# A two-block network on one core: the attention's value products moved beside another unit's scores, twelve fillers in its tail, wider sums in the opening, a token-major last block

## The reference

```python
for gi, (window, dilation) in enumerate(((128, 1), (512, 4), (2048, 16))):   # per group
    q = apply_partial_rope(proj[:, :, gi, 0], cos, sin) * scale
    k = apply_partial_rope(proj[:, :, gi, 1], cos, sin)
    o_g, lse_g = dilated_group_attention(q, k, proj[:, :, gi, 2], window, dilation)
wts = jax.nn.softmax(jnp.stack(lses, axis=0), axis=0)
o = jnp.einsum('gbsh,gbshd->bshd', wts, jnp.stack(outs, axis=0))
...
u = jax.nn.relu(rmsnorm(x, norm_ffn) @ w_ff1)
return x + (u * u) @ w_ff2
```

## Time and profile before

| | us |
|---|---|
| median of 3 runs | 3054.78 (3050.89 to 3054.91) |
| the profiled execution | 3049.26 |
| its span, first to last instruction | 3047.6 |
| PE busy | 3011.1 (99%) |
| DVE busy | 1563.9 (51%) |
| ACT busy | 1137.8 (37%) |

### The profile page before, as it was taken

How to read it: one execution, slowest core, us unless ns; L and a number is a source line. 1 busy time by engine, 2 the same in 40 slices (tenths; PEclk the granted TensorE clock), 3 DMA queues, 4 the chain that set the end, 5 groups by cost and what they waited for, 6 DMA issues and landing times.

```text
span 3047.6 us, 39602 instructions
## 1 busy us (share of the span) xinstructions
PE 3011.1 (99%) x16986; PEld 2529.7 (83%) x16986; DVE 1563.9 (51%) x2167; ACT 1137.8 (37%) x1683; POOL 30.3 (1%) x44
## 2 busy tenths in 40 slices
PE   7999999999999999999999999999999999999999
PEld 6888988888987777988889777888889877898887
DVE  7776654545165565633335755653334654663342
ACT  5654422224232333522225455342233455442231
POOL 0000000000000000000000000000000000000000
PEclk9999999999999999999999999999999999999999
DMA  8433354532332221232322221222222221222222
GB/s 298 163 117 106 121 197 152 189 119 84 97 92 67 68 75 61 67 97 97 97 89 87 83 70 57 82 98 96 98 96 90 84 83 64 81 91 97 97 97 83
DMA packets 219917, 311.59 MB, mean 102 GB/s; under 512 B 12032, under 2 KB 120544, under 8 KB 219744
## 3 DMA queue, kind: packets, MB, share of 16 engines
q1 hardware_dynamic: 208528, 267.01, 26.7%
q0 software_dynamic: 10880, 41.95, 3.9%
q10 hardware_dynamic: 336, 0.12, 0.0%
HBM read 306.93 MB, written 2.10 MB: 101 GB/s over the span
## 4 chain that ended last, share of the span: by engine, by line
PE 90%; DVE 7%; ACT 1%; issue 1%; DMA 0%; ACTq 0%; SPq 0%; DVEq 0%
PE G L2067 64%; PE G L2110 9%; PE G L2071 6%; DVE yT L1585 1%; PE X L2175 1%; PE X L2451 1%; DVE w_lo L1220 1%; PE G L2327 1%; PE G L2089 1%; PE X L2528 1%; PE X L2512 1%; PE X L2535 1%; PE X L2292 1%; PE X L2298 1%; PE X L2477 1%
## 5 line engine op out<-in xcount | busy, mean ns | idle before, releaser
L2067 PE MATMUL G<-u_hi,w_hi 128*128 128x512 f32 x2160 | 863.8, 400 | 0.0
L2067 PE MATMUL G<-u_hi,w_lo 128*128 128x512 f32 x2160 | 842.5, 390 | 0.0
L2067 PE MATMUL G<-u_lo,w_hi 128*128 128x512 f32 x2160 | 841.3, 389 | 0.0
L1220 DVE TENSOR_TENSOR w_lo<-raw,w_hi 128x2048 fp32r<-128x2048 f32 (+3 forms) x240 | 540.3, 2253 | 480.5 <-ACT w_hi L640 479.8
L640 ACT CAST w_hi<-raw 128x2048 fp32r<-128x2048 f32 (+3 forms) x242 | 454.6, 1880 | 526.6 <-DMA raw<-in_w_ff 242.4
L2067 PEld LDWEIGHTS G<-u_hi,w_hi 128*128 128x128 f32 x2160 | 405.5, 188 | 101.6 <-issue 18.2
L2067 PEld LDWEIGHTS G<-u_hi,w_lo 128*128 128x128 f32 x2160 | 405.3, 188 | 87.3
L2067 PEld LDWEIGHTS G<-u_lo,w_hi 128*128 128x128 f32 x2160 | 406.1, 188 | 80.1 <-issue 1.4
L2067 PE MATMUL G<-ff_hi,w_hi 128*128 128x512 f32 x448 | 174.9, 390 | 0.0
L2067 PE MATMUL G<-ff_hi,w_lo 128*128 128x512 f32 x448 | 174.4, 389 | 0.0
L2067 PE MATMUL G<-ff_lo,w_hi 128*128 128x512 f32 x448 | 174.3, 389 | 0.0
(11 more groups left out here) (427 smaller groups left out, 4379.6 us busy)
## 6 DMA issues: line engine op xcount, KB each, us to landing
raw<-in_w_ff SPq DMA_DIRECT2D x128, 512.0 KB, 4.4
raw<-in_ffn_w_in SPq DMA_DIRECT2D x88, 512.0 KB, 4.5
ada_raw<-in_ada_w POOLq DMA_DIRECT2D x40, 1024.0 KB, 6.6
raw<-in_w_in SPq DMA_DIRECT2D x56, 512.0 KB, 4.2
raw<-in_attn_w_in SPq DMA_DIRECT2D x96, 256.0 KB, 3.7
raw<-in_ffn_w_out SPq DMA_DIRECT2D x40, 512.0 KB, 4.8
raw<-in_hgrn_w_in SPq DMA_DIRECT2D x32, 512.0 KB, 4.5
raw<-in_attn_w_in SPq DMA_DIRECT2D x24, 512.0 KB, 4.2
```

The source lines that it names most:

```text
L1220: tt(w_lo[slot][:, 0:nk, 0:w], raw[slot][:, 0:nk, 0:w], w_hi[slot][:, 0:nk, 0:w].bitcast(F32), ALU.subtract).then_inc(s_lo, 1)
L2067: ins = mm(G[0:c1_ - c0, m, :], w[iw][:, k, c0:c1_], xs[ix][:, x0(b) + kk, :], start=first, stop=last, skip_group_check=True)
```

## The change

Four places.

1. Opening. Part 0 also leaves its first two k-rows to PE. The sums are 64 columns wide, parts 0 and 1 go to bank G3. Only the first of the four k-tiles of the first weight chunk is split before the adds, the others after; the same in halves for the second chunk. DVE writes `u_full` of tiles 0 and 4, ACT copies tiles 4 to 7 of x into `hT`. Tile 7 of the normed x goes through bank X3. The sum of part 3 comes after the first chunk.
2. Dilated attention. Values at +3, behind the next unit's scores and ahead of the transposes, groups 1 and 2 first and group 0 last; scaling at +4, output transpose at +5, copy at +6. Rotations at offsets 7, 8, 10, 11. In the tail 12 pieces of 6 matmuls: the first chunk of `at_out` in eight, and two of four k-tiles of the second in four. `out_last` does the last two k-tiles for all tiles.
3. Window attention. Values at +6, behind another unit's scores; copy at +7.
4. Last block. Its second half (features 512 to 1023) is token-major, and the residual enters its sum by four transposes of `hT` per tile. ACT copies a finished tile straight to `x_view`. Tiles 0 to 3 are transposed together at one tick. The output goes in one piece of 1 MB and four of 256 KB.

```diff
-        att_last = att_start(ATT_TILES - 1) + 8
+        att_last = att_start(ATT_TILES - 1) + 7
...
-        FIRST_ADA, FIRST_SUMS = (0, 2, 1, 3), (3, 2, 3, 2)
-        ON_PE = {1: 2, 2: 2}
+        FIRST_ADA, FIRST_SUMS = (0, 2, 1, 3), (G[:, 3, 0:256], G[:, 3, 256:512], X[:, 3, 0:256], X[:, 2, 0:256])
+        ON_PE = {0: 2, 1: 2, 2: 2}
+        FIRST_COLS = 64
...
-            pieces = ((0, 4), (4, 6), (6, 7), (7, 8))
-            for k0, k1 in pieces:
-                sp.wait_ge(s_res, k1)
...
+            sp.wait_ge(s_res, 4)
+            sp.dma_start(by_token[:, :, 0:512], x_view[:, :, 0:512]).then_inc(s_out, 16)
+            for j in range(TB):
+                sp.wait_ge(s_res, 5 + j)
+                sp.dma_start(by_token[:, j, 512:1024], x_view[:, j, 512:1024]).then_inc(s_out, 16)
...
+                if k % 4:
+                    sc.activation(u_full[:, k, :], tmp[:, k, :], ACT.Identity, **kw)
                 n.give(sc.activation(u_hi[:, k, :], tmp[:, k, :], ACT.Identity, **kw), s_uhi)
+                if k == 5:
+                    first_h((6, 7))
+                if k == 0:
+                    sc.copy(w_hi[0][:, 1:4, :], raw[0][:, 1:4, :]).then_inc(s_hi, 1)
+                    normed(7)
+                    act.wait_ge(s_free["act"], 4)
                 if k == 3:
+                    first_h((4, 5))
                     first_w(1)
...
-            first_products(0, range(8))
+            first_products(0, range(2, 8))
             first_products(1, range(2, 8))
+            n.take(st["first_k_upper"])
+            n.give(tt(w_lo[0][:, 0, :], raw[0][:, 0, :], w_hi[0][:, 0, :].bitcast(F32), ALU.subtract), st["first_k_lower"])
+            dve.wait_ge(s_asum, 2)
             first_add(0)
-            first_w(0)
             first_add(1)
             first_mix(0)
+            n.take(st["normed_copied"], 3)
+            first_x(0)
             first_u(0)
+            dve.wait_ge(s_hi, 1)
+            tt(w_lo[0][:, 1:4, :], raw[0][:, 1:4, :], w_hi[0][:, 1:4, :].bitcast(F32), ALU.subtract).then_inc(s_lo, 1)
...
-                        p, tau = divmod(T - 7 - 2 * j - part, ATT_TICKS)
+                        p, tau = divmod(T - 7 - 3 * j - part, ATT_TICKS)
...
-            OUT_TICKS = (97, 101, 104, 107)
+            OUT_TICKS = (97, 97, 100, 101, 103, 104, 106, 107, 109, 112, 114, 115)
...
+                        joined = spec is not None and name == order[-1]
+                        if joined and s == 0:
+                            for f in range(4):
+                                nc.tensor.matmul(G[:, m, blk(f)], hT[:, 4 + f, blk(m)], ident, start=f == 0, stop=False, is_transpose=True, skip_group_check=True)
...
-                for t in att_at(T, 6):
+                for t in att_at(T, 5):
...
+                for t in att_at(T, 3):
...
+                    pe.wait_ge(at["copied"], t + 1)
+                    for g in (1, 2):
+                        for r in range(4):
+                            mm(X[32 * r:32 * r + 32, t % 2, 0:P], pt[0:w1, P * (nb + g - 1) + 32 * r:P * (nb + g - 1) + 32 * r + 32],
+                               at_v[0:w1, r, cols(g)], start=g == 1, stop=False, skip_group_check=True, tile_position=(0, 32 * r))
+                    for j in range(nb):
+                        ins = mm(o, pt[:, blk(j)], at_v[:, i - nb + 1 + j, cols(0)], start=False, stop=j == nb - 1, skip_group_check=True)
+                    ins.then_inc(at["output"], 1)
...
-                for t in att_at(T, 4):
...
+            def out_piece(i):
...
+                s, m = (0, i // 2) if i < 8 else (1, i - 8)
+                k0 = 2 * (i % 2) if s == 0 else 0
...
+            def out_last():
...
+                for k in (2, 3):
+                    pe.wait_ge(split_done, base + 4 + k + 1)
+                    for m in range(4):
+                        for iw, ix in PASSES:
+                            ins = mm(G[:, m, :], w[iw][:, k, blk(m)], xs[ix][:, 4 + k, :], start=False, stop=(k, iw, ix) == (3, 1, 0), skip_group_check=True)
+                        if k == 3:
+                            ins.then_inc(s_tile, 1)
...
-                for u in win_at(T, 5):
...
+                for u in win_at(T, 6):
...
-                k = {24: 0, 25: 1, 26: 2, 27: 3, 30: 4, 31: 5}.get(t)
-                if k is not None:
-                    result_tile(k)
+                if t == 24:
+                    for k in range(4):
+                        result_tile(k)
```

More of the change, by code:

```diff
@@ L1287, in first_mix, with first_x @@
                 n.give(stt(mix[:, k0:k0 + 4], mod[:, 8 + k0:12 + k0], 1.0, cols_b[:, k0:k0 + 4], ALU.add, ALU.mult), st["mix"])
+            def first_x(k):
+                n.own(st["mix"])
+                link(ts(u_full[:, k, :], tmp[:, k, :], mix[:, k:k + 1], mod[:, k:k + 1], ALU.mult, ALU.add))
             def first_u(k):
@@ L2020, in linear @@
                         last_k_apart(name, b, x_hi, x_lo, x0, tick)
+                    elif name == "at_out" and b == 0:
+                        out_last()
                     else:
-                        plain(name, b, x_hi, x_lo, tiles, x0, range(1 if name == "at_out" and b == 0 else 0, g["chunks"]), tick=tick)
+                        plain(name, b, x_hi, x_lo, tiles, x0, range(g["chunks"]), tick=tick)
                     ada = ada_index(name, b)
@@ L2062, in plain @@
                                 for iw, ix in PASSES:
[L2063 removed]
+                                    first = kk == 0 and (iw, ix) == (0, 0) and (part is None or part is spec[0]) and not joined
                                     last = kk == last_k and (iw, ix) == (1, 0)
@@ L2502, in window @@
             def window(T):
-                for u in win_at(T, 5):
-                    t, i = divmod(u, 4)
-                    kv, keys = t // 2, keys_of(i)
-                    n.take(ws["copied"])
-                    if i == 0 and u:
-                        n.take(ws["done"])
-                    for j, kb in enumerate(keys):
-                        for a_ in range(2):
-                            ins = mm(X[64 * a_:64 * a_ + 64, 3, blk(i)], z_v[:, kb, 64 * kv:64 * kv + 64], win_pt[u % 2][:, blk(a_ * len(keys) + j)],
-                                     start=i == 0, stop=kb == i, skip_group_check=True, tile_position=(0, 64 * a_))
-                    if i == 3:
-                        n.give(ins, ws["output"])
                 for u in win_at(T, 0):
@@ L2530, in window @@
                     n.give(ins, ws["scores"])
+                for u in win_at(T, 6):
+                    t, i = divmod(u, 4)
+                    kv, keys = t // 2, keys_of(i)
+                    if i == 0 and u:
+                        n.take(ws["done"])
+                    for j, kb in enumerate(keys):
+                        for a_ in range(2):
+                            ins = mm(X[64 * a_:64 * a_ + 64, 3, blk(i)], z_v[:, kb, 64 * kv:64 * kv + 64], win_pt[u % 2][:, blk(a_ * len(keys) + j)],
+                                     start=i == 0, stop=kb == i, skip_group_check=True, tile_position=(0, 64 * a_))
+                    if i == 3:
+                        n.give(ins, ws["output"])
                 for u in win_at(T, 3):
```

153 lines of the change are left out of this document (93 added, 60 removed).

## The result

The changed kernel takes 3033.94 (median of 4 runs, 3033.12 to 3034.33) against 3052.84 for the kernel before beside it (4 runs, 3050.45 to 3054.91): ratio 0.9941, 95% interval 0.9928 to 0.9953. Forecast were 3034.5 and 3024 to 3045. The profiled execution took 3033.12, its span is 3031.4, 16.2 shorter than before.

The account below looks back on a forecast made before the run. TensorE (PE), busy 99% of the span, was taken as the bound. Gains of 2.0 + 8.8 + 5.0 + 3.6 + 1.1 = 20.5, taken from the median 3054.78, gave 3034.5, range 3024 to 3045.

Parts of the forecast that it names:

- Opening: Start of kernel: first projection at 27.3 instead of 30.49, second block at 57.4 instead of 59.41; gain 2.0.
- The chain that follows (ada sums, scans) has over 1 us to spare: After the opening: work behind the second block has over 1 us of slack, so the opening's 2.0 gain stands.
- Rival B: Opening: the clock falls at 25.2 despite 64-column sums; gain 19.1 in all, time 3035.7; chance 0.20.
- Like units: Attention under the projection: changeovers per unit fall from 0.58 to 0.15, 0.40 saved in each of 12 units.
- Unlike units: Attention under the projection, values of 32 or 64 rows: one more changeover of 0.12, so 0.28 saved in 13 units.
- the order's leftovers: Attention under the projection: an allowance that took the 8.4 from 25 units to 8.8.
- C: Unlike narrow tiles in attention and window pay 0.43 per changeover: 13 less, gain 7.4, time 3047.4; chance 0.12.
- E: Any step from scores to values drains PE; slower kernel, 3062.8 at 0.5 more per step; chance 0.03.
- Rival D: Output transposes under the projection wait 0.6 for DVE in each of 25 units: gain 5.5, time 3049.3; chance 0.05.
- Attention end: From unit 26's scores to the second block: 49.5 becomes 44.4, with stalls 1.6, 0.8 and 1.3; gain 5.0.
- Window: Window attention, values behind scores: 0.15 saved in 13 of 16 units, 0.05 lost in up to 3; 3.6 for two layers.
- Last block: Last block and output: last matmul 0.87 later, shorter way to the copy, output 0.2 faster; gain 1.1.

Follow-up runs that it names:

- e9: Changed kernel with the last four products of ada_w's eighth part over 16 of 512 columns; first scores 830.5 after the second block, no total time given.
- e10: Changed kernel with the attention end's three waits removed and the first window scores waiting only for the first half of the rotated queries; 3026.72, ratio 0.9916.
- e1: Changed kernel with opening sums one column wide in place of 64; second block starts at 58.30 against 58.76, no total time given.
- e2: Changed kernel with 24 more identity transposes issued before the first transposes of x; projection started at 29.92 against 29.20, no total time given.
- e4: Changed kernel with the narrow value products over 128 rows everywhere; the run took 3035.2.
- e3: Changed kernel with the values at their new place but full tiles first and narrow ones last; 3042.43, ratio 0.9967.
- e12: Kernel before, unchanged, run a third time for another profile; 3051.67.

## Why the prediction was right

Every part went the way that was forecast, and the time was right within 0.6, but the latter by errors that nearly cancel. The sum was 4.3 too large against the profiled executions (20.5 for 16.2). Against it, the kernel before usually runs 3 longer than in its profiled execution (3049.26, below all of its 32 timed ones, whose median is 3052.3), the changed kernel only 0.8; and the median that the gain was taken from, 3054.78, lies 1.9 above the one measured beside the change. That the time came so near is luck. (Less 20.5 that median is 3034.3, not the 3034.5 written, and the fifth k-tile's start adds up to 45.3, not 45.5.)

- **Opening, forecast 2.0.** The step that failed is "The chain that follows (ada sums, scans) has over 1 us to spare". The spare was 1.4 in the profile before, already less than the 2.0 that was to come off in front of it; it is 0.4 in the changed kernel's own profile and gone in six other executions [e9, e10]. e9 shows that VectorE's work ahead of the scans sets it; that the transfers of `ada_w` time that work is in part argued. The second block started 2.2 earlier in e10, and the first scores 0.1. In the profiles the first scores start at 889.79 to 891.69 with the opening of before (five) and at 889.31 to 891.87 with the new one (seven; e2 and e9 are left out): no difference that they show. Of the projection's 1.9 of lateness, 0.6 is a later start of that execution (the products began at 15.63, not 15.05); for the rest PE's own sums stood last (they ended at 26.8, not 25.1), since part 0's and most of the transposes behind them ran at the lower clock (3.68 and 4.76 long, in e10 2.00 and 3.55). e10 shows nearly the forecast's times where they didn't.
- **The clock.** With one column it fell at 24 to 26.3 in all six profiles. With 64 it held in seven of eight and fell in e10, behind a wait of 0.93 between the sums that the seven don't have. So the width made the difference in seven executions and was not enough in the eighth. Rival B's fall is real, but it costs nothing that reaches the first scores: e1 and e10 have it and start them at 889.45 and 889.79. The Trainium skill (TensorE: Matmul & The Clock Gate, Part 4) has transposes not counted as busy. e2 speaks against it once more: only transposes stood before the sixteen that ran 0.11 apart.
- **Like units, 0.40.** Measured 0.37. Narrow to full costs 0.22 in all (0.12 on the last narrow group, 0.10 on the first full matmul, and 0.08 on the projection less 0.08 ahead of it), not 0.15.
- **Unlike units, 0.28.** Measured 0.18 and 0.20. The changeover itself is 0.12 to 0.15 by e4, where 0.12 was assumed, and only 32 and 64 rows pay it. Twelve like units at 0.37 and thirteen unlike at 0.19 make the 6.9, where the forecast's prices make 8.4; the 0.4 that it added for "the order's leftovers" stood on no row and didn't come. Rivals C and E fall: C's place is right, at a third of its price. The Trainium skill (TensorEngine Tiling (Array Packing), Key Properties) has the array drained when the tiling mode changes, not when only the tile does. The runs agree: from 128 rows to 96 in narrow tiles nothing is paid, to 64 or 32 it is 0.12 to 0.15.
- **Rival D.** No wait of PE on the output transposes under the projection: the 0.6 of margin was enough.
- **Attention end, 5.0.** Waits are 3.2 where 3.7 were placed, but PE's own work is 42 and not 40.6: each of the twelve pieces starts with a matmul of 0.32 in place of 0.23, which is 1.0 of it.
- **Window, 3.6.** Measured 3.2. Per unit it is 0.13, where 0.15 was forecast, and 2.1 a layer up to the last unit's scores; 0.45 is then lost where the last units' values stand by themselves (0.15 was allowed).
- **Last block, 1.1.** With the forecast in brackets, eight transposes more cost 0.84 (0.87), the shorter way to the copy gives 1.85 (1.77), the output 0.28 (0.2, which no row of before had shown).

## What to carry to other kernels

Small matmuls of different tile shapes cost by the border, not by the piece: put the narrow ones of one unit directly behind the narrow ones of another, with rows that cost no changeover (96 beside 128 cost none, 32 and 64 did), and keep one passage to the full array. The same move with the full tiles first is worth 0.4 of 6.9 (e3). An earlier start is worth only what the next chain lets through: before it is counted, follow it to the next place where TensorE waits for work that hangs on a transfer. And take more than one profile of a kernel before a term of 1 us is read from it.

## What the runs showed of the hardware

- The clock column of a profile begins with its first change. In the changed kernel it reads 1.00 from the start, and yet the transposes at 10.61 stand 0.21 apart; distances tell the level there.
- Before a layer's first window scores PE waits 1.6 for VectorE (1.95 from one matmul's start to the next). In 5 of the 26 such places in thirteen profiles the granted clock fell within 2 behind the pause and stayed down for 3.4, at a cost of 1.6. The same kernel has it in one execution and not in the next.
- A granted clock that is up when x's transposes run can be down ten microseconds later. e2 had it up early and lost it at 16.8, in a pause of 1.93; e10 lost it at 25.2, behind a wait of 0.93, with sums of 64 columns.

Still open: why, in executions with the same instructions, the clock had risen by 15 in some (e10, before) and not until 22 in another (the changed kernel); how often the kernel before has the falls that e12 shows, which three profiles can't tell; and whether it was the wait of 0.93 that let the clock fall in e10, which no run tries alone.
